# Gate products handed out anew around the turned weights of a delta rule, on one Trainium2 core

## The reference

```
u, w   = solve(I + m, [v * beta, k_beta * exp(G)])      # per chunk of 64 tokens, 4 heads of 128
v_new  = u - w @ s
o      = q_dec @ s + qk @ v_new
s      = s * exp(gl) + k_tail^T @ v_new                 # the state, chunk after chunk
y      = (sigmoid(gA) * (o_a @ w_oa) + sigmoid(gB) * (o_b @ w_ob)) @ w_out
```

## Time and profile before

| | us |
|---|---|
| median of 3 runs | 1856.26 (1856.22 to 1856.89) |
| the profiled execution's own time | 1856.23 |
| its span, first to last instruction | 1854.5 |
| TensorE busy | 1809.7 (98%) |
| VectorE, ScalarE, GpSimd busy | 1404.0, 1123.3, 103.8 |
| layer 0, delta rule's gate products up to the merge's first product | about 150 to 257 |
| layer 1, the same | about 678 to 786 |

### The profile page before, as it was taken

One profiled execution on the slowest core, in us unless ns is written; L12 is line 12 of the kernel. 1 busy time (PEld: TensorE's weight loads), 2 busy tenths in 40 slices (PEclk: granted clock), 3 DMA queues, 4 the chain that ended last, 5 costly groups with the idle time before them and its releaser, 6 DMA issues.

```text
span 1854.5 us, 27361 instructions
## 1 busy us (share of the span) xinstructions
PE 1809.7 (98%) x11218; PEld 1546.3 (83%) x11218; DVE 1404.0 (76%) x1542; ACT 1123.3 (61%) x1249; POOL 103.8 (6%) x158
## 2 busy tenths in 40 slices
PE   8999999999999999999999999999999999999996
PEld 6879998999977889996888888888888888888875
DVE  5885377644348883575888988989888888898897
ACT  4465344444333573444777777777777777777774
POOL 5002000000031020001000000000000000000010
PEclk9999999999999999998999999999999999999998
DMA  7233284554431332472999999999999999999993
GB/s 202 69 101 99 69 239 137 159 161 174 142 87 46 99 121 71 120 233 85 361 360 373 390 374 377 385 361 389 377 378 390 364 383 375 371 390 375 377 393 148
DMA packets 263967, 468.39 MB, mean 253 GB/s; under 512 B 32625, under 2 KB 111681, under 8 KB 263838
## 3 DMA queue, kind: packets, MB, share of 16 engines
q1 hardware_dynamic: 260464, 459.55, 70.9%
q0 software_dynamic: 1824, 6.55, 0.9%
q10 hardware_dynamic: 1550, 0.48, 0.1%
HBM read 458.66 MB, written 7.90 MB: 252 GB/s over the span
## 4 chain that ended last, share of the span: by engine, by line
PE 51%; DVE 2%; ACT 1%; issue 1%; DVEq 0%; ACTq 0%
PE ps L364 50%; DVE wl L395 1%; ACT wh L389 1%; PE ps L707 0%; DVE resid L3027 0%; DVE hT L2661 0%; DVE resid L2715 0%; DVE resid L3032 0%; ACT gEh L2892 0%; DVE resid L786 0%; DVE resid L792 0%; ACT gEl L2894 0%; DVE resid L2689 0%; DVEq L2466 0%; PE ps L2835 0%
## 5 line engine op out<-in xcount | busy, mean ns | idle before, releaser
L395 DVE TENSOR_TENSOR wl<-ring,wh 128x2048 fp32r<-128x2048 f32 x385 | 879.9, 2291 | 209.3 <-ACT wh L389 206.0
L389 ACT ACTIVATE wh<-ring 128x2048 fp32r<-128x2048 f32 x385 | 739.9, 1924 | 273.2 <-PE ps L364 272.2
L364 PE MATMUL ps<-wh,xgh 128*128 128x512 f32 x896 | 355.3, 397 | 1.9 <-DVE xgl L2619 1.0
L364 PE MATMUL ps<-wh,xgl 128*128 128x512 f32 x896 | 349.5, 390 | 0.0
L364 PE MATMUL ps<-wl,xgh 128*128 128x512 f32 x896 | 348.9, 389 | 0.0
L364 PE MATMUL ps<-hPh,ringr 128*128 128x288 f32 x1024 | 228.8, 305 | 2.4 <-DVE ringr L446 2.3
L364 PEld LDWEIGHTS ps<-wh,xgh 128*128 128x128 f32 x896 | 168.3, 188 | 38.2 <-DVE wl L395 4.2
L364 PEld LDWEIGHTS ps<-wh,xgl 128*128 128x128 f32 x896 | 168.2, 188 | 36.0
L364 PEld LDWEIGHTS ps<-wl,xgh 128*128 128x128 f32 x896 | 168.5, 188 | 33.1
L364 PEld LDWEIGHTS ps<-hPh,ringr 128*128 128x128 f32 x1024 | 170.7, 190 | 8.9 <-issue 4.9
L364 PE MATMUL ps<-hPl,ringr 128*128 128x288 f32 x512 | 152.1, 297 | 0.0
(11 more groups left out here) (440 smaller groups left out, 2501.1 us busy)
## 6 DMA issues: line engine op xcount, KB each, us to landing
ring<-in_moe_w SPq DMA_DIRECT2D x336, 1024.0 KB, 7.6
ring<-in_w_in SPq DMA_DIRECT2D x38, 1024.0 KB, 5.2
ring<-in_ffn_w SPq DMA_DIRECT2D x33, 1024.0 KB, 5.3
ring<-in_w_out SPq DMA_DIRECT2D x8, 1024.0 KB, 9.9
ring<-in_w_in SPq DMA_DIRECT2D x32, 128.0 KB, 3.3
ring<-in_w_oa SPq DMA_DIRECT2D x16, 256.0 KB, 5.5
ring<-in_w_ob SPq DMA_DIRECT2D x8, 512.0 KB, 6.9
yrow<-ysb SPq DMA_DIRECT2D x7, 512.0 KB
```

What stands on the lines that cost most here:

```text
L364: ins = nc.tensor.matmul(*a, **k)
L389: nc.scalar.activation(wh[:, k % WS, :], ring[:, s:s + SLOT], ACT.Copy).then_inc(hi_ready, 1)
L395: ins = nc.vector.tensor_tensor(wl[:, k % WS, :], ring[:, s:s + SLOT], wh[:, k % WS, :].bitcast(F32), ALU.subtract)
```

## The change

Three entries of the table change, and the turned weights get a product behind each of their first four groups. ktok and MdT keep 7 products in place of 8. wT has 8 in place of 3: one behind each of the four groups of tiles 0 and 1, and four behind tile 2. The sum up to wT is 84 in place of 81; the steps keep their 28, and the last fill has 16 in place of 19. ScalarE's places for reading the gates follow from the same table: counted from 0, gates 4, 6 and 8 are read one of its rounds later (in front of P4, B and wT), and gate 13 in the steps instead of at the end.

```diff
-        FILL = {"grow": 8, "KK": 6, "ktok": 8, "MdT": 8, "QKT": 4, "MoT": 4, "P2": 2, "vtok": 2, "P2T": 2, "X1": 3, "P4": 2, "P4T": 2,
-                "X2": 3, "P8": 2, "X3": 3, "X3T": 3, "B": 3, "BT": 2, "Y1": 3, "B2": 2, "TT": 3, "u": 3, "wT": 3}
+        FILL = {"grow": 8, "KK": 6, "ktok": 7, "MdT": 7, "QKT": 4, "MoT": 4, "P2": 2, "vtok": 2, "P2T": 2, "X1": 3, "P4": 2, "P4T": 2,
+                "X2": 3, "P8": 2, "X3": 3, "X3T": 3, "B": 3, "BT": 2, "Y1": 3, "B2": 2, "TT": 3, "u": 3, "wT": 8}
         STEP_FILL = 4
+        W_FILL = 1
...
                         need("TT", i)
                         need("ktok", i)
                         w_turned(i, 0)
+                        fill(W_FILL)
                     for i in (0, 1):
                         need("u", i)
                         w_turned(i, 1).then_inc(prep_done, 1)
+                        fill(W_FILL)
                     need("TT", 2)
                     need("ktok", 2)
                     w_turned(2, 0).then_inc(prep_done, 1)
-                    fill(FILL["wT"])
+                    fill(FILL["wT"] - 4 * W_FILL)
                     assert filled[0] == filled_after("wT")
```

## The result

The changed kernel takes 1863.42 us in the median of 18 runs (1854.42 to 1865.71), the one before, beside it, 1856.32 (18 runs, 1855.07 to 1857.80). The ratio on record is 1.0035, 95% interval 1.0028 to 1.0042 (the quotient of the two medians is 1.0038). The forecast was 1856.0 within 1853.5 to 1858.2. The profiled execution of the changed kernel took 1862.09 us with a span of 1860.3; its mean granted clock is 0.989 where it was 0.991.

The account below looks back on a forecast made before the run. TensorE, busy 98%, was taken as the bound, with ScalarE's last split ending the block. Per layer -0.79 + 2.57 - 0.52 = +1.26 us before the steps, block end -0.12; twice that from 1856.23 gave 1856.0, range 1853.5 to 1858.2.

Parts of the forecast that it names:

- The entries: Turned weights, each layer: going in and out of a product costs about 0.20 us; 9.32 us up to the state product.
- The end of the block: Three products fewer in the last fill save 1.18 us, but the block ends only 0.12 us earlier a layer.
- VectorE's chain: From the last state gain to the split of the merge's first unit: moves by the whole +1.26 us, ending at 256.47.
- the stall before gate 15: In the last fill at 250.59, gate 15 waits for gate 13 to be read; its 0.27 us goes.
- The cover at ktok and MdT: Before the QKT round, 3.8 us are left after VectorE's products free its bank; costed at nothing.
- ScalarE's order: Gate 8's reading and pair 14's halving fall between copies of u and turned weights, about 2.3 us; costed at nothing.
- the DMAs: No load added; slots behind product 96 or 112 freed within 0.1 us of the old moment; no term in the sum.
- A rule against a row: Turned weights: thin passes lower the clock, a few dense products hold it, against the skill's idle-gap rule; falls cost 3.1 us.
- rows 3: Trace stretches 311.73 to 315.14 (TensorE busy 2.23 of 3.41 us) and 564.31 to 567.72 (thin passes, some products) keep the clock.
- Rival C: A wait costed at nothing opens, or stages behind shift against their half-clock stretches: up to 1 us either way; chance 0.07.
- Rival A: The clock still falls behind the turned weights: 1.56 us lost again a layer, 1859.1 (one layer alone 1857.6); chance 0.14.

Follow-up runs that it names:

- e5: Against the changed kernel: two products behind each of the four groups in place of one, none behind tile 2 (84 before the steps); 1856.87 us, ratio 1.0011.
- e3: Against the changed kernel: two products behind each of the four groups in place of one, 88 ahead of the steps; 1868.99 us, ratio 1.0066.
- e1: Against the changed kernel: no products between the turned weights, all eight behind them (the change's table alone); 1857.88 us, ratio 1.0008.

## Why the prediction was wrong

- **The entries: right.** 9.32 us was worked out for the stretch up to the state product, 9.30 measured where the clock stayed. At the block's end all of it comes to 1.26 us a layer, against 1.44. A fall of 3.41 us costs 1.51, against 1.56, and the turned weights begin 0.87 us earlier, against 0.79.
- **The end of the block: right.** Three products fewer there shorten almost nothing, since VectorE's chain moves with the steps, and the stall before gate 15 is gone. One detail differs: VectorE's split was to end 0.3 us behind ScalarE's, and the two ended within 0.04 us of each other.
- **The cover at ktok and MdT, ScalarE's order, the DMAs: right.** No gap appeared on TensorE from the rounds to the last state product in either profiled execution.
- **The step that failed** is the one under "A rule against a row": that "a few dense products hold" the clock and that the new stretch mixes as the rounds from 173 to 213 do. By it the forecast took 3.4 us at half clock away from each layer, 3.1 us of time in all. The runs show more half-clock time than before, 44.7 us against 33.4, and in three of four layers profiled the changed kernel's clock falls among its turned weights. One product behind each eight passes is not what the rounds have, which is two or three behind each forty. Pairs in the same place fell in none of four layers there, and in e5, the clean test, the half-clock time is 26.0. The argument from rows 3 made a rule of two places that keep the clock; what keeps it there no run tested.
- **A term that was put at nothing** failed beside it: what the new table does to the clock without any product between the turned weights. Rival C let the stages behind shift by up to 1 us in time. The table alone has 40.8 us at half clock against 33.4, worth 3.7 us, of which 1.2 come back in its rest. The single products were forecast to take half-clock time away; on top of the table they took none away, and cost 3.0 us of rest.
- **Rival A had the direction and the wrong size.** It charged one stretch of the old length in each layer (1859.1) and put longer ones at 0.03. The runs show 6.83, 6.83 and 10.24 us, all beginning with thin groups still to be done, which at half clock take 1.83 us in place of 1.03. Each 3.41 us costs 1.5. By the table of runs the changed kernel has 11.3 us more at half clock than the one before.
- **Luck, and one execution.** That both layers fell by the same 3.4 us in the profiled execution of the kernel before made the fall look like a fixed cost of the program. The second execution has it in one layer only.
- **The page's rule** that only idle gaps throw the clock back (the Trainium skill, "TensorE: Matmul & The Clock Gate", section "Why this matters for your kernels") gave a time nearer to the result by naming no cure, but the runs don't agree with it: TensorE was busy throughout in every window shown ahead of and in these stretches, and pairs in place of singles took 18.7 us of half-clock time away (14.6 by means over the runs).

What stays open: why the table alone brings earlier and more falls; how much of it the single products add on top; why pairs keep the clock through the turned weights and then lose it over the steps in e3; and why one product behind the thin run made two short stretches rather than a long one. No more than one or two executions of a kernel were profiled, and the others give only a mean clock.

## What to carry to other kernels

A run of small fp32 passes can cost TensorE its clock although it never idles; look at the granted clock behind each such run, and price a cure with the entries it adds and with a fall that it may only move or draw out. Shorten the thin run first (here by issuing the two row halves in turn), and if dense work is put into it, don't count on single products: here pairs kept the clock there and singles didn't, and neither was faster than nothing. When the time hangs on the clock, one profile is one throw: compare the mean clocks of many runs before the time of a change is believed or forecast.

## What the runs showed of the hardware

- Thirty-two passes of 64 rows by 128 columns took 3.32 us with the lower rows first and 1.93 us with lower and upper rows in turn, into different banks: 0.104 us a pass and 0.060. So passes with weights 128 columns wide run partly beside each other here if their rows differ.
- TensorE's granted clock fell to 1.2 GHz behind or inside runs of small fp32 passes although the engine had been busy all the time: for 4.33 of 4.33 us in the kernel before, for 3.27 of 3.27 in e1.
- The same binary ran from 1854.42 to 1865.71 us, 0.6% of its time. The Trainium skill says, in "TensorE: Matmul & The Clock Gate", section "What's actually happening", that the window in which the engine's activity is judged runs free of the kernel, so that executions of one kernel differ. The runs agree in that they differ, and the fall came 6.54 and 5.60 us behind the start of layer 0's turned weights in two executions of the changed kernel.
- Every half-clock stretch shown above was 3.41, 6.83 or 10.24 us long.
